# First attention of a two-block network: the probability pipeline made one step deeper

## The chip, the cores and the metric

The kernel runs on one core of one Trainium2 chip, in one launch. The metric is device time in microseconds (us), lower is better. The core has five engines that run their own instruction streams and meet only at semaphores: TensorE (PE: matrix products and transposes), VectorE (DVE), ScalarE (ACT), GpSimd (POOL) and SyncE (SP, which here only issues transfers).

## The reference

The network has two blocks on one sequence of 512 tokens and 1,024 features: a recurrent and convolutional mixer with a retrieval layer, and then two attention layers, each with a SwiGLU. The change concerns only the first attention, which has 16 heads of 64 features in 4 groups. Each head's output is a gated sum of three attentions (cut to what matters; all eight key blocks are selected, so "sel" is a full causal attention):

```python
p_cmp = softmax(q @ k_cmp + bias)      # 31 compressed keys
p_sel = softmax(q @ k_sel + bias)      # all keys up to the query
p_win = softmax(q @ k_win + bias)      # the last 256 keys
g = sigmoid(gl + b_gate)               # (tokens, heads, 3)
o = g[..., 0:1] * (p_cmp @ v_cmp) + g[..., 1:2] * (p_sel @ v_sel) + g[..., 2:3] * (p_win @ v_win)
```

## The kernel before

**Items and steps.** Heads are handled in pairs ("half" 0 and 1), eight pairs ("items") in all. Each pair takes four steps, one for each tile of 128 queries, `qt` = 0 to 3, so there are `STEPS` = 32 steps. A step's size follows `qt`: the sel scores are 128, 256, 384 and 512 wide, the win scores 128, 256, 384 and 384, and the cmp scores 31. Below, "step 3" is a step with `qt` = 3, and "iteration i" is the turn of an engine's loop whose `s` has `qt` = i.

**The work of a step s**, in the order in which data flows through it:
1. `scores(s)` on TensorE: six products (three branches for two heads) into PSUM banks 0 to 3. There is one set of these banks, so each product waits until DVE has read the last step's (`bank_read`).
2. `row_max(s)` on DVE: six reductions that add the bias, write to the probability buffer `pA[s % 3]` in SBUF and give the row maxima (L1611).
3. `exponentials(s)` on ACT: six Exp instructions in place, with row sums (L1664).
4. `inverse(s)` on DVE: the inverted sums times the gates, three small instructions (L1627, L1629, L1633), which raise `inv_ready`.
5. `scale(s)` on DVE: three multiplications for half 0 (L1640: sel, win, cmp) and one for half 1 (L1644: sel). At the same time GpSimd does half 1's win and cmp (L1696).
6. `turn(s)` on TensorE: the scaled probabilities are transposed block by block into PSUM banks 4, 5 and 7, in chunks of four blocks (L1556). Step 0 has 4 wide blocks, step 1 has 8, step 2 has 12 and step 3 has 14, and each has two narrow cmp blocks; that gives 2, 3, 4 and 4 chunks. A chunk may be written only when the chunk three before it in the running count has been copied out of the same bank.
7. The copies of the chunks to SBUF (`ptA`, two buffers): all but a step's last chunk by ACT (`copies`, L1589), the last chunk by DVE (`last_copy`, L1592, and for step 3 first L1589, since its last chunk has two wide blocks too).
8. `values(s)` on TensorE: products of values and turned probabilities (L1570). After an item's step 3 ACT drains the output (`drain`, L1678).

**The order is written by hand.** An engine runs its own list strictly in order:
- TensorE in iteration s: `scores(s+1)`, `values(s-2)`, `turn(s-1)`.
- DVE in iteration s: `row_max(s)`, `last_copy(s-2)`, `inverse(s-1)`, `scale(s-1)`.
- ACT in iteration s: `exponentials(s)`, `copies(s-1)`, `drain` if step s-2 ended an item.

Before the first of DVE's reductions stands one tiny copy (L381). When the attention ends, the output projection begins on TensorE (L563).

Of the kernel before, what the change touches and what calls it, by code (L numbers as in the profile page):

```python
# [21 lines left out]
P = 128  # L22
ALU = mybir.AluOpType
ACT = mybir.ActivationFunctionType
# [139 lines left out]
def program(nc, t):  # L164

    with ExitStack() as ctx:
# [123 lines left out]
        cin = wide.take(2, CMP_POS // 2, NKV * NCMP + 1)  # L290
        hid_bias = wide.take(2, 2, 1)
        a2 = Region(after)
        pA, ptA = a2.take(3, 2 * 928), a2.take(2, 16 * P)
        mxA, denA, invA = a2.take(3, 2, 3), a2.take(3, 2, 3), a2.take(3, 2, 3)
# [1202 lines left out]
        DVE_ORDER = (("sel", 0), ("win", 0), ("cmp", 0), ("sel", 1), ("win", 1), ("cmp", 1))  # L1497
        READS_BEFORE = (1, 4, 3, 6, 3, 6)
        SCORES_BEFORE = (1, 5, 5, 2, 6, 6)

# [33 lines left out]
        def nsa_pe(pe):  # L1534
# [6 lines left out]
                        pe.wait_ge(LA.bank_read, PER * (s - 1) + READS_BEFORE[x])  # L1541
                    pe.matmul(b.scores, b.q, b.keys, start=True, stop=True).then_inc(LA.scores_ready, 1)  # L1542

            def turn(s):
                for c, chunk in enumerate(turn_chunks(s)):
                    no = chunk_no(s) + c
                    turns = len(TURN_BANKS)
                    if no - turns in bank_of:
                        chunk_copied(pe, *bank_of[no - turns])
                    bank_of[no] = s, c  # L1550
                    other = max(half for half, _ in chunk)
                    pe.wait_ge(LA.scaled, 2 * s + 1 + other)
                    if other:
                        pe.wait_ge(LA.scaled_rest, s + 1)
                    for x, (_, (at, width, _)) in enumerate(chunk):
                        tr = pe.transpose(ps[0:width, turn_bank(no), P * x:P * x + P], pA[:, s % 3, at:at + width], ident)  # L1556
                    tr.then_inc(LA.turned, 1)

            def values(s):
# [24 lines left out]

# [9 lines left out]

        def nsa_dve(dve, step):

            def row_max(s):

                it, qt = divmod(s, TT)
                if qt == 0:  # L1600
                    dve.wait_ge(LA.tab_in[it % 2], 16 * 2 * (it // 2 + 1))
                if s >= 3:
                    dve.wait_ge(LA.turned, chunk_no(s - 2))
                    dve.wait_ge(LA.exp_done, s - 2)
                if s:
                    dve.wait_ge(LA.bank_read, PER * s)
                apart(dve)
                for x, (name, half) in enumerate(DVE_ORDER):
                    b = branches(s, half)[name]
                    dve.wait_ge(LA.scores_ready, PER * s + SCORES_BEFORE[x])  # L1610
                    dve.tensor_tensor_reduce(  # L1611
                        out=pA[:, s % 3, b.at:b.at + b.width], in0=b.scores, in1=b.tab, scale=1.0, scalar=-FLOOR,
                        op0=ALU.add, op1=ALU.min,
                        accum_out=mxA[:, s % 3, half, b.slot:b.slot + 1]).then_inc(LA.bank_read, 1)

            def last_copy(s):
                c = len(turn_chunks(s)) - 1
                dve.wait_ge(LA.turned, chunk_no(s + 1))
                if s >= 2:
                    dve.wait_ge(LA.pv_done, s - 1)  # L1620
                copy_chunk(dve.tensor_copy, s, c, LA.last_copied)

            def inverse(s):
                it, qt = divmod(s, TT)
                dve.wait_ge(LA.exp_done, s + 1)
                den, inv = denA[:, s % 3], invA[:, s % 3]
                step.do(dve.tensor_scalar(den, den, 1e-30, None, ALU.max))  # L1627
                step.settle()
                step.do(dve.reciprocal(inv, den))  # L1629
                step.settle()  # L1630
                h0 = heads(it)[0]
                gates = gateA[:, qt, :].rearrange("p (a b) -> p a b", b=3)[:, h0:h0 + GR + 1:GR, :]
                dve.tensor_tensor(inv, inv, gates, ALU.mult).then_inc(LA.inv_ready, 1)  # L1633

            def scale(s):
                sides = [branches(s, half) for half in range(2)]
                dve.wait_ge(LA.inv_ready, s + 1)
                for b in sides[0].values():
                    pr = pA[:, s % 3, b.at:b.at + b.width]
                    ins = dve.tensor_scalar(pr, pr, invA[:, s % 3, 0, b.slot:b.slot + 1], None, ALU.mult)  # L1640
                ins.then_inc(LA.scaled, 1)
                b = sides[1]["sel"]
                pr = pA[:, s % 3, b.at:b.at + b.width]
                dve.tensor_scalar(pr, pr, invA[:, s % 3, 1, 1:2], None, ALU.mult).then_inc(LA.scaled, 1)  # L1644

            for s in range(STEPS + 2):
                if s < STEPS:
                    row_max(s)
                if s >= 2:
                    last_copy(s - 2)  # L1650
                if 1 <= s <= STEPS:
                    inverse(s - 1)
                    scale(s - 1)

        def nsa_act(act):

            def exponentials(s):
                if s >= 3:
                    act.wait_ge(LA.inv_ready, s - 2)
                for half in range(2):  # L1660
                    act.wait_ge(LA.bank_read, PER * s + 3 * half + 3)
                    for b in branches(s, half).values():
                        pr = pA[:, s % 3, b.at:b.at + b.width]
                        ins = act.activation(pr, pr, ACT.Exp, bias=mxA[:, s % 3, half, b.slot:b.slot + 1], scale=-1.0,  # L1664
                                             accum_out=denA[:, s % 3, half, b.slot:b.slot + 1])
                ins.then_inc(LA.exp_done, 1)

            def copies(s):
# [9 lines left out]
                act.copy(attn[:, it, :].rearrange("p (a t) -> p a t", a=TT),  # L1678
                         bank(OUT_BANK).rearrange("p (a t) -> p a t", a=TT)[:, :, ::-1]).then_inc(LA.o_drained, 1)

            for s in range(STEPS + 2):
                if s < STEPS:
                    exponentials(s)
                if 1 <= s <= STEPS:
                    copies(s - 1)
                if s >= 2 and (s - 2) % TT == TT - 1:
                    drain((s - 2) // TT)

        def nsa_pool(pool):

            for s in range(STEPS):
                pool.wait_ge(LA.inv_ready, s + 1)
                side = branches(s, 1)
                for b in (side["win"], side["cmp"]):
                    pr = pA[:, s % 3, b.at:b.at + b.width]
# [1359 lines left out]
```

## Time and profile before

| | us |
|---|---|
| median of three runs | 2896.09 |
| lowest and highest | 2893.24, 2896.78 |
| span of the profiled execution | 2893.6 |
| first matmul of the first attention's scores, from the span's start | 1605.67 |
| first matmul after the first attention | 1761.23 |

The page of the profile gives the profiled execution by its span, 2893.6 us; no separate time for what lies around it is listed. "Busy" is the time in which an engine executes; a matmul's end is modelled, so a busy TensorE may still be waiting inside a group. A group's start is that of its first instruction; the distance from one group's start to the next one's start is what the first really took on its engine. In brackets behind a row stands the idle time ahead of it and what ended that.

### The profile page before, as it was taken

Reading aid. Unit: us, or ns where it says so; the run is one execution under the profiler, and the core shown is the slowest. Engines: PE = TensorE matmul, PEld = TensorE weight load, DVE = VectorE, ACT = ScalarE, POOL = GpSimd, SP = SyncE. Lnnn points to the kernel's source line nnn. Section 1 sums busy time; section 2 is a strip of 40 time slices with the busy share of each in tenths; the row PEclk is TensorE's granted clock in tenths of the full one; section 3 lists DMA queues with packets and bytes.
Section 4 is the critical chain, followed back from the end, with each engine's and each line's share of the span. In section 5 each row is a group of like instructions: output and inputs, shape, how many; then the busy total and the mean of one; then the engine's idle time right before and its main releaser. Section 6 shows DMA issues by size and latency. Waiting matters only on the chain.

```text
span 2893.6 us, 35834 instructions
## 1 busy us (share of the span) xinstructions
PE 2703.8 (93%) x12080; PEld 1725.0 (60%) x12080; DVE 1888.1 (65%) x4922; ACT 845.0 (29%) x1654; POOL 1183.9 (41%) x837
## 2 busy tenths in 40 slices
PE   8998999999877877799999999999999999999999
PEld 3374454444323322244447777888888877788887
DVE  8998788888888888778766896544223336554411
ACT  4732211111111111121123785222232127522222
POOL 5314444444444444344440233444434434444443
PEclk9999999999999999999999999999999999999999
DMA  4169999999999999999997221232323222222332
GB/s 131 61 236 370 420 412 421 420 420 420 422 421 410 415 421 412 421 419 420 420 420 239 60 69 54 97 97 94 107 87 100 92 68 66 66 95 95 102 101 79
DMA packets 130309, 700.39 MB, mean 242 GB/s; under 512 B 16694, under 2 KB 28886, under 8 KB 64343
## 3 DMA queue, kind: packets, MB, share of 16 engines
q0 software_dynamic: 74352, 543.04, 45.6%
q1 hardware_dynamic: 54760, 153.30, 16.0%
q10 hardware_dynamic: 1072, 2.41, 0.2%
q8 instruction: 75, 1.23, 0.2%
q14 instruction: 50, 0.41, 0.0%
HBM read 696.41 MB, written 2.28 MB: 241 GB/s over the span
## 4 chain that ended last, share of the span: by engine, by line
PE 49%; DMA 19%; issue 14%; DVE 9%; POOL 7%; ACT 1%; POOLq 0%; DVEq 0%; SPq 0%; ACTq 0%
DMA arena<-in_peer_uv,arena 18%; PE ps L543 16%; PE ps L883 14%; POOL w_lo L420 6%; PE ps L2363 3%; DVE arena L1216 2%; PE ps L911 2%; PE ps L795 1%; PE ps L1556 1%; PE ps L1570 1%; DVE arena L1227 1%; PE ps L852 1%; PE ps L1542 1%; PE ps L2023 1%; DMA ring<-in_a_in 1%
## 5 line engine op out<-in xcount | busy, mean ns | idle before, releaser
L883 PE MATMUL ps<-arena 128*128 128x512 f32 x2048 | 952.0, 609 | 145.6 <-DVE arena L1227 144.7
L1350 POOL DMA_INDIRECT arena<-in_peer_uv,arena x512 | 568.9, 1111 | 785.6 <-PE ps L883 723.8
L883 PEld LDWEIGHTS ps<-arena 128*128 128x128 f32 x2048 | 380.8, 192 | 653.2 <-issue 383.2
L1216 DVE CUSTOM_DVE_ANT_0 arena<-arena,sq 128x1024 f32<-128x1024 f32 x512 | 607.1, 1223 | 195.0 <-DMA arena<-in_peer_uv,arena 190.8
L420 POOL TENSOR_TENSOR w_lo<-ring,w_hi 128x1024 fp32r<-128x1024 f32 (+1 forms) x156 | 407.2, 2610 | 514.9 <-ACT w_hi L433 514.9
L543 PE MATMUL ps<-n_hi,w_hi 128*128 128x512 f32 x992 | 387.5, 391 | 0.5 <-issue 0.3
L543 PE MATMUL ps<-n_hi,w_lo 128*128 128x512 f32 x992 | 386.0, 389 | 0.0
L543 PE MATMUL ps<-n_lo,w_hi 128*128 128x512 f32 x992 | 381.9, 389 | 0.2 <-DVE n_lo L470 0.2
L1043 ACT ACTIVATE dots_gel<-dots_gel,tok_scale 128x2 f32<-128x2 f32 x256 | 75.6, 295 | 1006.7 <-DVE dots_gel L1216 1006.6
L433 ACT CAST w_hi<-ring 128x1024 fp32r<-128x1024 f32 (+1 forms) x156 | 174.6, 1119 | 644.3 <-PE ps L543 644.3
L543 PEld LDWEIGHTS ps<-n_hi,w_hi 128*128 128x128 f32 x992 | 186.2, 188 | 40.9 <-issue 2.4
L543 PEld LDWEIGHTS ps<-n_lo,w_hi 128*128 128x128 f32 x992 | 186.2, 188 | 40.1 <-DVE n_lo L470 0.8
L543 PEld LDWEIGHTS ps<-n_hi,w_lo 128*128 128x128 f32 x992 | 186.2, 188 | 38.5
L1227 DVE TENSOR_SCALAR arena<-consts,dots_gel,tcmp 128x128 f32<-128x128 f32 x512 | 160.4, 365 | 29.2 <-ACT dots_gel L1043 13.8
L599 DVE TENSOR_TENSOR h<-ps,h 128x512 f32<-128x512 f32 x32 | 22.1, 691 | 218.9 <-PE ps L543 218.9
L1425 DVE TENSOR_TENSOR arena<-ps,rstd 128x512 f32<-128x512 f32 x44 | 30.4, 692 | 200.4 <-PE ps L543 200.4
L543 PE MATMUL ps<-hid_hi,w_hi 128*128 128x512 f32 x352 | 137.1, 389 | 1.3 <-POOL w_lo L420 1.3
L543 PE MATMUL ps<-hid_lo,w_hi 128*128 128x512 f32 x352 | 137.0, 389 | 0.0
L543 PE MATMUL ps<-hid_hi,w_lo 128*128 128x512 f32 x352 | 136.9, 389 | 0.0
L2363 PE MATMUL ps<-n,ring 128*128 128x512 f32 x256 | 113.9, 602 | 8.2 <-DMA ring<-in_w_in 7.5
L1696 POOL TENSOR_SCALAR arena<-arena 128x384 f32<-128x384 f32 (+2 forms) x64 | 53.1, 839 | 163.2 <-DVE arena L1633 163.2
L911 PE MATMUL ps<-n,ring 128*128 128x384 f32 x320 | 111.9, 486 | 0.0
(366 smaller groups left out, 3619.2 us busy)
## 6 DMA issues: line engine op xcount, KB each, us to landing
ring<-in_a_up SPq DMA_DIRECT2D x44, 512.0 KB, 3.5
ring<-in_b_up SPq DMA_DIRECT2D x44, 512.0 KB, 3.5
ring<-in_a_in SPq DMA_DIRECT2D x40, 512.0 KB, 7.2
ring<-in_b_q SPq DMA_DIRECT2D x24, 512.0 KB, 3.4
ring<-in_a_down SPq DMA_DIRECT2D x16, 704.0 KB, 3.9
ring<-in_b_down SPq DMA_DIRECT2D x16, 704.0 KB, 4.0
ring<-in_w_in SPq DMA_DIRECT2D x16, 512.0 KB, 3.7
arena<-in_peer_uv,arena POOLq DMA_INDIRECT x512
```

The lines of the kernel that those rows point to most:

```text
L420: pool.tensor_tensor(w_lo[:, j % 2, 0:kt * P], ring[:, j, 0:kt * P], w_hi[:, j % 2, 0:kt * P], ALU.subtract).then_inc(split_lo, 1)
L433: act.copy(w_hi[:, j % 2, 0:kt * P], ring[:, j, 0:kt * P]).then_inc(split_hi, 1)
L543: mm = pe.matmul(bank(j // 2 if two else j), w[:, j % 2, cols], r[:, x, :], start=no == 0 and not (two and j % 2), stop=no == len(passes) ...
L883: mm = pe.matmul(bank(2 * (tt % 2) + q), diag[:, no % DIAGS, r, :], uvrow[p][r][:, D + 512 * q:D + 512 * q + 512], start=slot + r == 0, st ...
L911: mm = pe.matmul(ps[:, p % 2, 0:EARLY], ring[:, p % RING, k * P:(k + 1) * P], n[:, k, 0:EARLY], start=k == 0, stop=k == DK - 1)
L1043: act.activation(gel[:, p, :], dots[:, p, :], ACT.Gelu_apprx_tanh, scale=tok_scale[:, tt:tt + 1]).then_inc(gel_ready, 1)
L1216: ins = dve.tensor_tensor_reduce(out=u, in0=u, in1=ntok[:, tt, :], scale=1.0, scalar=0.0, op0=ALU.mult, op1=ALU.add, accum_out=dots[:, p, ...
L1227: ins = dve.tensor_scalar(diag[:, no % DIAGS, r, :], ident, gel[:, p, r:r + 1], gate_now[:, slot + r:slot + r + 1], ALU.mult, ALU.mult)
L1350: pool.indirect_dma_start(uvrow[p][r], None, t["peer_uv"], bass.IndirectOffsetOnAxis(ap=expert_id[:, tt, slot + r:slot + r + 1], axis=0)). ...
L1425: dve.tensor_tensor(gated[:, pr, :], bank(2 * pr + 1), rstd[:, :], ALU.mult).then_inc(tile_drained, 1)
L1696: ins = pool.tensor_scalar(pr, pr, invA[:, s % 3, 1, b.slot:b.slot + 1], None, ALU.mult)
L2363: mm = pe.matmul(bank(u % RING), ring[:, u % RING, k * P:(k + 1) * P], ns[k], start=k == 0, stop=k == DK - 1)
```

## The change

Four probability buffers instead of three; the transposes of a step run one iteration later than before, and are split in two parts around the values and the scores; GpSimd takes half 1's sel and win instead of its win and cmp; DVE takes both halves' cmp in one `tensor_tensor`; DVE's reductions of half 1 come behind the last chunk's copy. The new orders are:
- TensorE in iteration s: `turn(s-2, 0)` (the chunks with blocks of half 0 only), `values(s-3)`, `scores(s+1)`, `turn(s-2, 1)` (the others).
- DVE in iteration s: `row_max(s, 0)`, `last_copy(s-3)`, `row_max(s, 1)`, `inverse(s-1)`, `scale(s-1)`.
- ACT in iteration s: `exponentials(s)`, `drain` if step s-3 ended an item, `copies(s-2)`.

```diff
+        SLOTS_A = 4
-        pA, ptA = a2.take(3, 2 * 928), a2.take(2, 16 * P)
+        pA, ptA = a2.take(SLOTS_A, 2 * 928), a2.take(2, 16 * P)
...
-            def turn(s):
+            def turn(s, later):
                 for c, chunk in enumerate(turn_chunks(s)):
+                    other = max(half for half, _ in chunk)
+                    if other != later:
+                        continue
                     no = chunk_no(s) + c
                     turns = len(TURN_BANKS)
                     if no - turns in bank_of:
                         chunk_copied(pe, *bank_of[no - turns])
                     bank_of[no] = s, c
-                    other = max(half for half, _ in chunk)
-                    pe.wait_ge(LA.scaled, 2 * s + 1 + other)
+                    pe.wait_ge(LA.scaled, s + 1)
                     if other:
                         pe.wait_ge(LA.scaled_rest, s + 1)
...
             scores(0)
-            for s in range(STEPS + 2):
+            for s in range(STEPS + 3):
+                if 2 <= s <= STEPS + 1:
+                    turn(s - 2, 0)
+                if s >= 3:
+                    values(s - 3)
                 if s + 1 < STEPS:
                     scores(s + 1)
-                if s >= 2:
-                    values(s - 2)
-                if 1 <= s <= STEPS:
-                    turn(s - 1)
+                if 2 <= s <= STEPS + 1:
+                    turn(s - 2, 1)
...
             def scale(s):
-                sides = [branches(s, half) for half in range(2)]
+                side = branches(s, 0)
                 dve.wait_ge(LA.inv_ready, s + 1)
-                for b in sides[0].values():
-                    pr = pA[:, s % 3, b.at:b.at + b.width]
-                    ins = dve.tensor_scalar(pr, pr, invA[:, s % 3, 0, b.slot:b.slot + 1], None, ALU.mult)
-                ins.then_inc(LA.scaled, 1)
-                b = sides[1]["sel"]
-                pr = pA[:, s % 3, b.at:b.at + b.width]
-                dve.tensor_scalar(pr, pr, invA[:, s % 3, 1, 1:2], None, ALU.mult).then_inc(LA.scaled, 1)
-
-            for s in range(STEPS + 2):
+                for b in (side["sel"], side["win"]):
+                    pr = pA[:, s % SLOTS_A, b.at:b.at + b.width]
+                    dve.tensor_scalar(pr, pr, invA[:, s % SLOTS_A, 0, b.slot:b.slot + 1], None, ALU.mult)
+                pr = pA[:, s % SLOTS_A, :].rearrange("p (h c) -> p h c", h=2)[:, :, 896:896 + NCMP]
+                dve.tensor_tensor(pr, pr, invA[:, s % SLOTS_A, :, 0:1].broadcast_to([P, 2, NCMP]), ALU.mult).then_inc(LA.scaled, 1)
+
+            for s in range(STEPS + 3):
                 if s < STEPS:
-                    row_max(s)
-                if s >= 2:
-                    last_copy(s - 2)
+                    row_max(s, 0)
+                if s >= 3:
+                    last_copy(s - 3)
+                if s < STEPS:
+                    row_max(s, 1)
                 if 1 <= s <= STEPS:
                     inverse(s - 1)
                     scale(s - 1)
...
-            for s in range(STEPS + 2):
+            for s in range(STEPS + 3):
                 if s < STEPS:
                     exponentials(s)
-                if 1 <= s <= STEPS:
-                    copies(s - 1)
-                if s >= 2 and (s - 2) % TT == TT - 1:
-                    drain((s - 2) // TT)
+                if s >= 3 and (s - 3) % TT == TT - 1:
+                    drain((s - 3) // TT)
+                if 2 <= s <= STEPS + 1:
+                    copies(s - 2)
...
                 side = branches(s, 1)
-                for b in (side["win"], side["cmp"]):
-                    pr = pA[:, s % 3, b.at:b.at + b.width]
-                    ins = pool.tensor_scalar(pr, pr, invA[:, s % 3, 1, b.slot:b.slot + 1], None, ALU.mult)
+                for b in (side["sel"], side["win"]):
+                    pr = pA[:, s % SLOTS_A, b.at:b.at + b.width]
+                    ins = pool.tensor_scalar(pr, pr, invA[:, s % SLOTS_A, 1, b.slot:b.slot + 1], None, ALU.mult)
                 ins.then_inc(LA.scaled_rest, 1)
```

## Rows read from the trace of the kernel before

**Rows 1.** The page: the span.

```profile
span 2893.6 us, 35834 instructions
```

**Rows 2.** Windows: one item of four steps; busy us of each engine, granted clock, DMA.

```profile
1657.90:1676.50 18.60, 18.00 (x187) 13.90 (x187) 16.93 (x87) 15.98 (x59) 6.62 (x9) 1.00 0.16 54
```

**Rows 3.** Chain of waits: start us, us, what; first scores, and first turn of a step 2.

```profile
1605.67 0.86 PE ps L1542 x12
...
1620.66 1.77 PE ps L1556 x14
```

**Rows 4.** Timeline of TensorE, one item: start us, us, line, shape, [idle before].

```profile
1676.49 1.77 PE L1556 MATMUL ps<-consts,arena 128*128 128x128 f32 x14 [0.50 <-DVE arena L1640]
1678.19 1.27 PE L1542 MATMUL ps<-arena 64*128 64x256 f32 x12
1679.39 1.91 PE L1570 MATMUL ps<-arena 128*64 128x128 f32 x28
1681.23 2.05 PE L1556 MATMUL ps<-consts,arena 128*128 128x128 f32 x16
1683.20 1.70 PE L1542 MATMUL ps<-arena 64*128 64x384 f32 x12
1684.83 2.12 PE L1570 MATMUL ps<-arena 128*64 128x128 f32 x32
1686.89 0.88 PE L1556 MATMUL ps<-consts,arena 128*128 128x128 f32 x6
1687.69 1.91 PE L1542 MATMUL ps<-arena 64*128 64x512 f32 x12
1689.54 1.02 PE L1570 MATMUL ps<-arena 128*64 128x128 f32 x12
1690.49 1.31 PE L1556 MATMUL ps<-consts,arena 128*128 128x128 f32 x10
1691.73 1.46 PE L1542 MATMUL ps<-arena 64*128 64x128 f32 x12
1693.13 1.46 PE L1570 MATMUL ps<-arena 128*64 128x128 f32 x20
1695.10 1.07 PE L1556 MATMUL ps<-consts,arena 128*128 128x128 f32 x8 [0.51 <-DVE arena L1640]
```

**Rows 5.** Timeline of the last two steps and the stage's end.

```profile
1750.93 1.77 PE L1556 MATMUL ps<-consts,arena 128*128 128x128 f32 x14 [0.64 <-DVE arena L1640]
...
1755.47 2.02 PE L1556 MATMUL ps<-consts,arena 128*128 128x128 f32 x16
...
1757.53 0.42 DVE L1589 COPY arena<-ps 128x256 f32<-128x256 f32 x1 [1.94 <-PE ps L1556]
...
1758.42 2.12 PE L1570 MATMUL ps<-arena 128*64 128x128 f32 x32 [0.93 <-DVE arena L1592]
...
1761.23 4.13 PE L563 MATMUL ps<-sq,ring 128*128 128x512 f32 x9 [0.69 <-ACT sq L1678]
```

**Rows 6.** Timeline of ACT: a copy, the drain, a step 3's first Exp, the next copy.

```profile
1687.64 0.59 ACT L1589 COPY arena<-ps 128x512 f32<-128x512 f32 x1 [1.54 <-PE ps L1556]
1688.12 0.59 ACT L1678 COPY sq<-ps 128x512 f32<-128x512 f32 x1
...
1692.55 0.73 ACT L1664 ACTIVATE arena<-arena 128x512 f32<-128x512 f32 x1
...
1695.82 0.59 ACT L1589 COPY arena<-ps 128x512 f32<-128x512 f32 x1
```

**Rows 7.** Chain of waits near the stage's end: from ACT's copies to TensorE.

```profile
1751.66 1.57 ACT arena L1589 x3
1753.23 0.25 issue
```

**Rows 8.** Line L1644 on DVE: duration ns min/median/max, forms.

```profile
L1644 DVE TENSOR_SCALAR arena<-arena x32: 274/514/687, 1611.0 to 1754.9; 128x128 f32<-128x128 f32 x8, 128x256 f32<-128x256 f32 x8, 128x384 f32<-128x384 f32 x8, 128x512 f32<-128x512 f32 x8
```

**Rows 9.** One step's scaling: timelines of DVE and GpSimd, GpSimd's wide instruction by form.

```profile
1674.78 1.56 DVE L1640 TENSOR_SCALAR arena<-arena 128x384 f32<-128x384 f32 x3
...
1674.84 1.94 POOL L1696 TENSOR_SCALAR arena<-arena 128x384 f32<-128x384 f32 x2 [3.14 <-DVE arena L1633]
...
L1696 POOL TENSOR_SCALAR arena<-arena 128x384 f32<-128x384 f32 x1 | 1.5, 1470 | 3.1 <-DVE arena L1633 3.1
```

**Rows 10.** GpSimd by form, whole kernel: the same operation 512 wide, another line.

```profile
L1873 POOL TENSOR_SCALAR arena<-arena 128x512 f32<-128x512 f32 x8 | 14.9, 1856 | 6.4 <-DVE arena L1856 6.4
```

More of the change, by code:

```diff
@@ L292, in program @@
         a2 = Region(after)
-        pA, ptA = a2.take(3, 2 * 928), a2.take(2, 16 * P)
-        mxA, denA, invA = a2.take(3, 2, 3), a2.take(3, 2, 3), a2.take(3, 2, 3)
+        SLOTS_A = 4
+        pA, ptA = a2.take(SLOTS_A, 2 * 928), a2.take(2, 16 * P)
+        mxA, denA, invA = (a2.take(SLOTS_A, 2, 3) for _ in range(3))
         onehot, rowbuf = low[:, 3, :], skT.rearrange("p a b -> p (a b)")
@@ L1496, in program @@
         PE_ORDER = (("sel", 0), ("sel", 1), ("win", 0), ("win", 1), ("cmp", 0), ("cmp", 1))
-        DVE_ORDER = (("sel", 0), ("win", 0), ("cmp", 0), ("sel", 1), ("win", 1), ("cmp", 1))
         READS_BEFORE = (1, 4, 3, 6, 3, 6)
@@ L1555, in turn @@
                     for x, (_, (at, width, _)) in enumerate(chunk):
-                        tr = pe.transpose(ps[0:width, turn_bank(no), P * x:P * x + P], pA[:, s % 3, at:at + width], ident)
+                        tr = pe.transpose(ps[0:width, turn_bank(no), P * x:P * x + P], pA[:, s % SLOTS_A, at:at + width], ident)
                     tr.then_inc(LA.turned, 1)
@@ L1595, in nsa_dve, with row_max @@
         def nsa_dve(dve, step):
-            def row_max(s):
+            def row_max(s, half):
                 it, qt = divmod(s, TT)
[L1600 to L1608, printed above, removed]
+                if not half:
+                    if qt == 0:
+                        dve.wait_ge(LA.tab_in[it % 2], 16 * 2 * (it // 2 + 1))
+                    if s >= SLOTS_A:
+                        dve.wait_ge(LA.turned, chunk_no(s - SLOTS_A + 1))
+                        dve.wait_ge(LA.exp_done, s - SLOTS_A + 1)
+                    if s:
+                        dve.wait_ge(LA.bank_read, PER * s)
+                    apart(dve)
+                for x, name in enumerate(("sel", "win", "cmp")):
                     b = branches(s, half)[name]
-                    dve.wait_ge(LA.scores_ready, PER * s + SCORES_BEFORE[x])
+                    dve.wait_ge(LA.scores_ready, PER * s + SCORES_BEFORE[3 * half + x])
                     dve.tensor_tensor_reduce(
-                        out=pA[:, s % 3, b.at:b.at + b.width], in0=b.scores, in1=b.tab, scale=1.0, scalar=-FLOOR,
+                        out=pA[:, s % SLOTS_A, b.at:b.at + b.width], in0=b.scores, in1=b.tab, scale=1.0, scalar=-FLOOR,
                         op0=ALU.add, op1=ALU.min,
-                        accum_out=mxA[:, s % 3, half, b.slot:b.slot + 1]).then_inc(LA.bank_read, 1)
+                        accum_out=mxA[:, s % SLOTS_A, half, b.slot:b.slot + 1]).then_inc(LA.bank_read, 1)
             def last_copy(s):
@@ L1625, in inverse @@
                 dve.wait_ge(LA.exp_done, s + 1)
-                den, inv = denA[:, s % 3], invA[:, s % 3]
+                den, inv = denA[:, s % SLOTS_A], invA[:, s % SLOTS_A]
                 step.do(dve.tensor_scalar(den, den, 1e-30, None, ALU.max))
@@ L1657, in exponentials @@
             def exponentials(s):
-                if s >= 3:
-                    act.wait_ge(LA.inv_ready, s - 2)
+                if s >= SLOTS_A:
+                    act.wait_ge(LA.inv_ready, s - SLOTS_A + 1)
                 for half in range(2):
@@ L1662, in exponentials @@
                     for b in branches(s, half).values():
-                        pr = pA[:, s % 3, b.at:b.at + b.width]
-                        ins = act.activation(pr, pr, ACT.Exp, bias=mxA[:, s % 3, half, b.slot:b.slot + 1], scale=-1.0,
-                                             accum_out=denA[:, s % 3, half, b.slot:b.slot + 1])
+                        pr = pA[:, s % SLOTS_A, b.at:b.at + b.width]
+                        ins = act.activation(pr, pr, ACT.Exp, bias=mxA[:, s % SLOTS_A, half, b.slot:b.slot + 1], scale=-1.0,
+                                             accum_out=denA[:, s % SLOTS_A, half, b.slot:b.slot + 1])
                 ins.then_inc(LA.exp_done, 1)
```

2 lines of the change are left out of this document (1 added, 1 removed).

## The prediction

> **What bounds the kernel now.** I read the page's span first [rows 1]: 2893.6 us, 0.1% under the median of the runs (2896.09), so a difference worked out on the span can be added to the median as it stands. Then the chain of waits, for where the stage lies: from the first scores at 1605.67 [rows 3] to the next stage's first matmul at 1761.23 [rows 5] are 155.56 us. All the rest of the kernel is untouched, so the change can move 5% of the time at most.
>
> The stage is periodic. A step 2's turn starts at 1620.66 [rows 3], and the last item's at 1750.93 [rows 5]: seven periods of 18.61 us. The windows [rows 2] show that nobody is far from full in one: TensorE 18.00 busy of 18.60, DVE 16.93, ACT 15.98, GpSimd 6.62, and the clock at its upper level. But a busy TensorE hides waits inside its groups, so I take what each group costs from the distance between starts [rows 4]:
> - turns: 1.70 (step 2), 1.97 (step 3), 0.80 (step 0), 1.24 (step 1), together 5.71. A chunk of four wide blocks is 0.49 (1.97 / 4).
> - values: 1.84 (step 2), 2.06 (step 3), 0.95 (step 0), 1.46 (step 1), together 6.31.
> - scores: 1.20 (step 1, 1,086 columns), 1.63 (step 2, 1,598), 1.85 (step 3). Step 0's took 1.40 for only 574 columns; at 0.84 ns a column, the slope of the first two, it would take 0.77. The other 0.63 is waiting for DVE's reads of the banks. Unheld sum: 5.45.
>
> So TensorE has 17.47 us of work in a period. The other 1.14 us are that 0.63 and the 0.51 in which step 2's turn waits for DVE's scaling [rows 4]. That is all a deeper pipeline can win: 1.14 x 7 = 8.0 us, if it adds no wait of its own.
>
> **The change part by part.** A turn one iteration later no longer waits for scaling: minus 0.51. DVE reads half 1's scores while TensorE does values, so the next scores aren't held: minus 0.63. Now what the new order makes late.
>
> (a) *The last chunk's copy.* Before, scores (0.8 to 1.9 us) stood between the turn of a step's last chunk and its values, and hid the copy. Now the last chunk comes at the end of an iteration, and the next begins with `turn(s-2, 0)` and then these same values. Step 0 has no chunk of half 0 alone (its four wide blocks are two of each half), so in iteration 2 nothing stands between step 3's last chunk and step 3's values. The trace has this very sequence once, at the stage's end, where TensorE had nothing else to do: turn at 1755.47, two copies by DVE, values at 1758.42 after 0.93 us idle [rows 5]. Plus 0.93 per period. In the other iterations there is one copy less (some 0.3 less, so 0.6) against one chunk of 0.49 as cover: 0.1 to 0.15 each, where no longer wait swallows it.
>
> (b) *ACT's order.* ACT does the copies of step s-2 behind the Exps of step s, and the Exps of step s+1 behind those copies. Count from the end of step 3's last chunk, T = 0, with every duration from the rows. TensorE: wait 0.93, values(3) 2.06, scores(3) 1.85, first chunk of step 0 0.49: at 5.33. Only then can ACT copy this chunk, since it was turned in the late part. ACT: 0.10 to see it (the copy in rows 5 follows the end of its turn by less), 0.48 from copy to next instruction [rows 6], six Exps of step 3 in 3.27 (1692.55 to 1695.82) [rows 6], then step 1's first copy 0.59 and 0.25 until TensorE moves on an ACT copy (1753.23 to 1753.48) [rows 7]: 10.02. TensorE needs this copy, because step 2's first chunk goes to the bank of step 1's first chunk (three back). On its own path it would be there at 5.33 + 0.31 (rest of step 0's turn) + 0.49 + 0.15 + 0.95 + 0.77 + 0.75 = 8.75. Plus 1.27 per period, the largest term, and a new one: behind the waiting transpose stand values(1) and scores(1), and DVE and ACT live on those scores.
>
> (c) *The rest of the period.* Chunk 0.49, values(1) 1.46, scores(1) 1.20, rest of step 2's turn 1.21: 14.38. Step 3's first chunk needs the bank of step 2's second chunk, turned at 13.66 and copied at 13.66 + 0.10 + 0.59 + 0.25 = 14.60: plus 0.22, which covers (a) in this iteration. Then 0.49, values(2) 1.84, scores(2) 1.63, rest of step 3's turn 1.48: 20.04. Check: 17.47 + 0.93 + 0.15 + 1.27 + 0.22 = 20.04.
>
> (d) *DVE and GpSimd.* L1644 goes: 32 instructions with a median of 514 ns [rows 8], some 2 us a period. It lies beside TensorE's values and turns now, DVE has 1.7 us idle a period already [rows 2], and in the new chain (a to c) DVE appears only with its copies: priced at nothing. If DVE were the bound it would be worth up to 16 us. The joint cmp `tensor_tensor` has 62 columns for 31; the trace has no such form. From below, it costs what the narrow multiplication does now. From above: in the step shown DVE's three L1640 end at 1676.34 and GpSimd's first, 384 wide, at 1674.84 + 1.47 = 1676.31 [rows 9]; the narrow one, last of the three, is done only when GpSimd's is. GpSimd's first becomes step 3's sel, 512 wide, 1.86 for 1.47 [rows 9, 10]: up to 0.4 us more a period on DVE. I take this upper end, and it still costs nothing: about 2 us saved, 0.4 given back. GpSimd's own pair of step 3 takes 1.86 + 1.47 = 3.3 us and is needed a whole iteration later; at 0.39 for each 128 columns, the difference of the two, its four pairs make 9.8 us a period, of 18.6.
>
> The Trainium skill, "SBUF — State Buffer", section "Who interferes with whom", says that DVE and GpSimd share one port pair as an exclusive lock, and that a `tensor_tensor` with both inputs in SBUF contends with GpSimd's reads. By that the new instruction is held exactly as the old one; the ends 1676.34 and 1676.31 agree [rows 9]. By the rule the hold is the 0.4 of above, without it 0; the sum is the same either way, because DVE is off the chain.
>
> (e) *The ends.* The fourth buffer itself costs nothing. From the last item's first chunk of step 2 to the next stage's first matmul: before 10.30 [rows 5]; after 0.49 + 1.46 + 1.21 + 0.22 + 0.49 + 1.84 + 1.48 + 0.93 + 2.81 (values of step 3 to L563, 1758.42 to 1761.23) = 10.9. From the first scores to the first chunk of step 2: before 14.99; after it follows ACT's four first sets of Exps and one copy, by my estimate 14.5, give or take 1. The ends cancel to +0.1.
>
> Sum: 7 x (20.04 - 18.61) + 0.1 = +10.1 us, so 2906.2.
>
> **The rivals.**
> - *Only the copy is exposed* (a without b). If ACT's excursion were 1.3 us shorter than I add up, or DVE's relief let the Exps start early, the period would be 17.47 + 0.93 + 3 x 0.15 = 18.85, and the time +1.7, 2897.8: no change. For it: (b) is a sum of small latencies and I have each from one place. Against: the order on ACT is fixed, and step 3's Exps can't start before step 0's chunk is turned.
> - *It is what a deeper pipeline should be* (the other side). TensorE never waits: 17.47 a period, minus 8.0, plus 0.1: 2888.2. One mechanism decides: that the last chunk is copied within the time of what stands ahead of its values. It would have to take under 0.49 us, and nothing at all in iteration 2; the 0.93 in rows 5 speaks against it. Only if unheld matmuls run faster than the distances in rows 4 say could this come out.
> - *GpSimd's wider work holds DVE.* If the joint cmp waited for both of GpSimd's instructions (3.3 us instead of 1.9) in step 3, DVE would be 1.4 late for step 1's first reductions and step 2's last copy, where I count some 0.4 of slack: 1 us a period more, +17, 2913. For it: the lock-like ends in rows 9. Against: there the narrow one waited for the first only.
> - *It does nothing*: the waits removed and made cancel. That is the first rival's number.
>
> **How the numbers follow.** My forecast 0.62 (2903 to 2909.5: 0.1 to 0.2 us on each of the four latencies, seven times, and the ends' 1 us); exposed copy only 0.18; faster 0.08; held by GpSimd 0.07; the rest, 0.05, beyond either end. Predicted time 2906. The range 2897 to 2912 takes in the forecast and the first rival. A measurement can tell about 0.2% (5.8 us) from no change. Slower: 0.57 of the forecast's 0.62, the GpSimd case, and half of the rest: 0.67. Same: 0.18, 0.05 and 0.01: 0.24. Faster 0.09.
>
> **What the new profile would show.** The distance of the first chunks of step 2 from item to item: 20.0 (18.85 or 17.5 for the rivals). Idle of 0.9 ahead of step 3's values, released by DVE's copy; about 1.3 ahead of step 2's first chunk, released by ACT's copy (L1589's place); no wait for scaling, and scores of step 0 in about 0.8. On ACT a wait of over 1 us for step 0's chunk ahead of step 3's Exps. DVE busy down by some 1.5 a period with more idle, GpSimd busy up to about 10 a period. I am wrong if that wait on ACT is missing, or if TensorE's groups are shorter than their distances here.

## The result and the profile after

The changed kernel takes 2905.63 us (median of five runs, 2903.45 to 2908.45) against 2896.09 (with two more executions of the kernel before, five in all, the median is the same and the lowest is 2890.80). The ratio is 1.0038, 95% interval 1.0028 to 1.0049: slower by 8 to 14 us. The profiled execution spans 2901.3 us. That is only 7.7 over the one of before, because the untouched part ahead of the stage happened to be 4.3 us shorter (first scores at 1601.33 for 1605.67); over all profiled kernels here that start lies anywhere from 1601.3 to 1605.7. So I compare the stage itself, from the first scores to the next stage's first matmul: 1768.98 - 1601.33 = 167.65 us for 155.56, or +12.1.

Timeline of TensorE in the changed kernel, a little over one item (L1558 is the turn, L1572 values, L1542 scores; it answers to [rows 4]):

```profile
1687.07 2.12 PE L1572 MATMUL ps<-arena 128*64 128x128 f32 x32 [0.93 <-DVE arena L1596]
1689.12 1.91 PE L1542 MATMUL ps<-arena 64*128 64x512 f32 x12
1690.97 1.31 PE L1558 MATMUL ps<-consts,arena 128*128 128x128 f32 x10
1692.39 1.03 PE L1572 MATMUL ps<-arena 128*64 128x128 f32 x12
1693.35 0.86 PE L1542 MATMUL ps<-arena 64*128 64x128 f32 x12
1694.14 0.88 PE L1558 MATMUL ps<-consts,arena 128*128 128x128 f32 x6
1696.05 0.66 PE L1558 MATMUL ps<-consts,arena 128*128 128x128 f32 x4 [1.03 <-ACT arena L1593]
1696.64 1.47 PE L1572 MATMUL ps<-arena 128*64 128x128 f32 x20
1698.03 1.27 PE L1542 MATMUL ps<-arena 64*128 64x256 f32 x12
1699.24 1.99 PE L1558 MATMUL ps<-consts,arena 128*128 128x128 f32 x14
1701.26 1.91 PE L1572 MATMUL ps<-arena 128*64 128x128 f32 x28
...
1707.19 2.13 PE L1572 MATMUL ps<-arena 128*64 128x128 f32 x32 [0.93 <-DVE arena L1596]
```

The period is 1707.19 - 1687.07 = 20.12 us, for 18.61. The two waits in brackets are the two that the prediction named. The first, ahead of step 3's values, ends with DVE's copy of the last chunk. The second, ahead of step 2's first chunk, ends with ACT's copy of step 1's. Scores of step 0 now take 0.79 (1693.35 to 1694.14), for 1.40 before, and no wait of TensorE's ends with scaling.

Timeline of ACT in the changed kernel (L1669 Exps, L1593 copies, L1683 drain; it answers to [rows 6]):

```profile
1689.53 0.56 ACT L1683 COPY sq<-ps 128x512 f32<-128x512 f32 x1
1691.72 0.59 ACT L1593 COPY arena<-ps 128x512 f32<-128x512 f32 x1 [1.62 <-PE ps L1558]
1692.20 0.73 ACT L1669 ACTIVATE arena<-arena 128x512 f32<-128x512 f32 x1
...
1695.42 1.05 ACT L1593 COPY arena<-ps 128x512 f32<-128x512 f32 x2
```

ACT stands idle for 1.62 us until step 0's chunk is turned, and only then starts step 3's Exps; step 1's copies, for which TensorE waits, follow 3.22 us later.

Windows of one item in the changed kernel (the columns of [rows 2]):

```profile
1669.01:1689.12 20.11, 17.98 (x188) 13.76 (x186) 15.94 (x82) 16.15 (x59) 9.03 (x9) 1.00 0.17 48
```

DVE is busy for 1.0 us less and idle for 4.2; GpSimd is busy for 2.4 more. TensorE and ACT work as much as before and wait more.

The end, from the last item's first chunk of step 2 to the next stage, took 12.58 us (1756.40 to 1768.98), for 10.30 before. Timeline and windows (the third number from the end is TensorE's granted clock as a share of 2.4 GHz) of the changed kernel there:

```profile
1756.40 1.12 PE L1558 MATMUL ps<-consts,arena 128*128 128x128 f32 x4 [1.82 <-ACT arena L1593]
1757.45 2.48 PE L1572 MATMUL ps<-arena 128*64 128x128 f32 x20
...
1756.00:1757.40 1.40, 1.00 (x4) 0.72 (x4) 1.30 (x5) 0.83 (x2) 1.40 (x2) 0.60 0.00 0
1757.40:1759.80 2.40, 2.40 (x21) 1.87 (x20) 0.34 (x2) 0.59 (x1) 2.40 (x2) 0.52 0.02 7
```

With no more scores to do, TensorE idled for 1.82 us, and behind that its clock was granted at half, 1.2 GHz, until 1759.7: values(1) took 2.41 us instead of 1.40. The idle alone doesn't decide it: in e5_narrow the same group stood behind the same 1.82 us of idle, and the clock stayed at 1.00.

### The profile page after: what moved, and what is told of

The parts are those of the page before. It is cut to its first block, busy times and chain, and to the rows that moved or that the text cites. A ratio compares the mean times of both kernels' runs of the same rounds, so it can differ in the third digit from the quotient of the medians.

```text
span 2901.3 us, 35800 instructions
## 1 busy us (share of the span) xinstructions
PE 2707.6 (93%) x12080; PEld 1726.6 (60%) x12080; DVE 1879.3 (65%) x4890; ACT 846.3 (29%) x1654; POOL 1204.7 (42%) x837
## 3 DMA queue, kind: packets, MB, share of 16 engines
q10 hardware_dynamic: 1072, 2.41, 0.3%
## 4 chain that ended last, share of the span: by engine, by line
PE 49%; DMA 19%; issue 14%; DVE 8%; POOL 7%; ACT 2%; POOLq 0%; DVEq 0%; ACTq 0%; SPq 0%
DMA arena<-in_peer_uv,arena 18%; PE ps L544 16%; PE ps L884 14%; POOL w_lo L421 6%; PE ps L2368 3%; DVE arena L1217 3%; PE ps L912 2%; PE ps L1572 2%; PE ps L1558 1%; PE ps L1542 1%; DVE arena L1228 1%; PE ps L796 1%; ACT arena L1669 1%; PE ps L2028 1%; PE ps L774 1%
## 5 line engine op out<-in xcount | busy, mean ns | idle before, releaser
L1701 POOL TENSOR_SCALAR arena<-arena 128x128 f32<-128x128 f32 (+3 forms) x64 | 72.3, 1140 | 150.6 <-DVE arena L1638 150.6
```

Source lines behind the costliest of these rows:

```text
L1701: ins = pool.tensor_scalar(pr, pr, invA[:, s % SLOTS_A, 1, b.slot:b.slot + 1], None, ALU.mult)
```

## The experiments

Every ratio is against the kernel before in runs on the same chip. "Period" is the distance between the scores of step 3 in two items, "stage" is as above. The kernel before had medians of 2892.7 to 2893.4 us beside the experiments, so rows are compared by their ratios, not by their times. Period and stage are of one profiled execution each. Six of these had some microseconds at half clock in the stage: the changed kernel, e4_early0 and e6_oldscale near its end, e7_mid, e8_deep_oldscale and e9_tail in the first item. So a difference of up to 3 us between two stages can be the clock's; the periods, taken from later items, are free of it.

| kernel | us | ratio (95%) | period | stage |
|---|---|---|---|---|
| before | | | 18.61 | 155.6 |
| changed | 2905.63 | 1.0038 (1.0028 to 1.0049) | 20.12 | 167.7 |
| e1_deeper | 2891.29 | 1.0000 (0.9991 to 1.0009) | 18.07 | 153.9 |
| e2_split | 2901.81 | 1.0027 (1.0015 to 1.0038) | 19.73 | 164.6 |
| e3_between | 2904.69 | 1.0039 (1.0025 to 1.0052) | 20.12 | 166.1 |
| e4_early0 | 2902.91 | 1.0029 (1.0019 to 1.0040) | 19.76 | 165.2 |
| e5_narrow | 2904.47 | 1.0041 (1.0025 to 1.0056) | 20.12 | 166.5 |
| e6_oldscale | 2908.02 | 1.0053 (1.0040 to 1.0067) | 20.35 | 170.0 |
| e7_mid | 2895.20 | 1.0005 (0.9996 to 1.0014) | 18.62 | 158.3 |
| e8_deep_oldscale | 2897.40 | 1.0017 (1.0007 to 1.0026) | 18.40 | 159.1 |
| e9_tail | 2889.98 | 0.9991 (0.9982 to 1.0000) | 18.08 | 152.0 |
| e10_early | 2891.84 | 0.9997 (0.9988 to 1.0006) | 18.56 | 154.7 |

**e1_deeper: the depth with the old orders.**

```diff
-                if 2 <= s <= STEPS + 1:
-                    turn(s - 2, 0)
-                if s >= 3:
-                    values(s - 3)
                 if s + 1 < STEPS:
                     scores(s + 1)
+                if s >= 3:
+                    values(s - 3)
                 if 2 <= s <= STEPS + 1:
-                    turn(s - 2, 1)
+                    turn(s - 2)
```

and on DVE `row_max(s, 0)`, `row_max(s, 1)`, `last_copy(s - 3)`.

> The changed kernel with the old orders one step deeper: TensorE in iteration s does scores(s+1), values(s-3), turn(s-2) whole; DVE does both halves of row_max(s), then last_copy(s-3). Four buffers and the new scaling stay. My theory (the cost is the place of the last chunk's copy and of ACT's Exps behind step 0's copy): scores stand between a last chunk and its values again, so the 0.93 us idle ahead of step 3's values goes; ACT still waits for step 0's chunk ahead of step 3's Exps, and TensorE then waits some 0.7 us for step 1's copies ahead of values(1). Period 17.5 + 0.7 = 18.2 us, stage some 3 us shorter than in the kernel before, time about 2893. Rival (depth itself or the new scaling is what costs): period stays near 20, time about 2905.

Measured: period 18.07, 2 us under that of the changed kernel. The depth isn't what costs, the order is. (The edit takes back two orders at once, TensorE's and DVE's split reductions; they weren't separated.) The 0.93 us are gone inside a period. The time falls back to that of the kernel before, not 3 us under it: of the 3.8 us that seven shorter periods give, the end takes 3.5 back (1755.29 - 1734.11 = 21.18 us from the last scores of step 3 to the next stage, for 1761.23 - 1743.53 = 17.70 before). The stage of the profile is 1.7 us shorter; I had 3. Timeline of TensorE, e1_deeper, a period and the last items:

```profile
1689.39 1.47 PE L1570 MATMUL ps<-arena 128*64 128x128 f32 x20 [0.41 <-ACT arena L1589]
...
1743.61 1.47 PE L1570 MATMUL ps<-arena 128*64 128x128 f32 x20 [1.91 <-ACT arena L1589]
1745.01 1.80 PE L1556 MATMUL ps<-consts,arena 128*128 128x128 f32 x14
1747.67 1.91 PE L1570 MATMUL ps<-arena 128*64 128x128 f32 x28 [0.87 <-ACT arena L1589]
1749.51 2.05 PE L1556 MATMUL ps<-consts,arena 128*128 128x128 f32 x16
1752.48 2.12 PE L1570 MATMUL ps<-arena 128*64 128x128 f32 x32 [0.93 <-DVE arena L1592]
```

Ahead of values(1) TensorE waits 0.41 (I had 0.7), and at the end, without scores between, every values pays for its copies.

**e2_split: the new scaling alone, in the kernel before** (the diff of `scale` and `nsa_pool`, with `s % 3`, and of `turn`'s wait for the scaling).

> The kernel before with the new division of the scaling alone (GpSimd sel and win of half 1, one tensor_tensor for both cmp), no depth. My theory: DVE gains about 0.35 us in each scaling and reaches step 2's scaling earlier, but the turn right behind it must now wait for GpSimd's two wide instructions (2.7 us for step 2, 3.1 for step 3): about 0.7 and 0.6 us of wait a period against 0.51 before, and 0.35 less of waiting in scores. Period 18.9 to 19.0 us, time 2898 to 2900. Rival (DVE is the bound, so its relief is a gain): period 18.0 or less, time under 2892. Rival (the scaling is the whole loss of the change): period 20, time 2905.

Measured: period 19.73, 0.7 over my forecast's upper end. TensorE waited for GpSimd 0.91 us at the second chunk of step 2 and 0.64 at that of step 3, as bracketed by the timeline of e2_split:

```profile
1698.59 1.28 PE L1556 MATMUL ps<-consts,arena 128*128 128x128 f32 x10 [0.91 <-POOL arena L1694]
...
1704.15 1.50 PE L1556 MATMUL ps<-consts,arena 128*128 128x128 f32 x12 [0.64 <-POOL arena L1694]
```

The place was right, the sizes too small: by the distances of starts the two turns took 1.05 and 0.76 us more than their work, where I had 0.7 and 0.6. Another 0.15 stood ahead of that turn of step 2, for DVE, and 0.27 in the scores of step 0. By itself the new scaling costs three quarters of what the whole change does (9.0 us of stage for 12.1), but in the changed kernel no wait ends with it; the losses don't add.

**e3_between: the early chunk's copy between the halves' Exps.**

```diff
                 for half in range(2):
...
+                    if not half and s >= 2 and (s - 2) % TT:
+                        copies(s - 2, [0])
...
```

(`copies` now takes the chunks to be copied, and its usual call leaves the early one out.)

> The changed kernel, but ACT copies the early chunk (the first one of steps 1 to 3) between the Exps of the two halves instead of behind both. Theory 'bank': TensorE's wait of 1.1 us ahead of step 2's first chunk is for that bank alone, so it goes: period 19.0 us, time about 2898. Theory 'ACT is late' (mine): the wait is gone from there, but values(1) right behind it need step 1's second copy, which ACT does behind all Exps of step 3; it only moves by 0.5 us of copy. The wait reappears ahead of values(1), 1.2 us long; period 20.0 to 20.2, time 2904 to 2906.

Measured: same time and period as the changed kernel. The bank came free, but the wait didn't move whole to values(1), as I had it: it split in two. Timelines of TensorE and of DVE's last scaling of step 2, e3_between:

```profile
1698.97 0.63 PE L1558 MATMUL ps<-consts,arena 128*128 128x128 f32 x4 [0.38 <-DVE arena L1647]
1700.16 1.47 PE L1572 MATMUL ps<-arena 128*64 128x128 f32 x20 [0.56 <-ACT arena L1593]
...
1698.61 0.21 DVE L1647 TENSOR_TENSOR arena<-arena 128x62 f32<-128x62 f32 x1
```

Step 2's first chunk still waits 0.38 us, now for DVE's scaling of step 2, and values(1) wait 0.56 for ACT, where I had 1.2. In the changed kernel this scaling ends at 1695.03 + 0.21 = 1695.24. By the 0.15 us from its end to the chunk here, it alone would have held the chunk until 1695.39, so 0.45 of the 1.11 us hide a second wait behind the one for ACT. But values(1) start at almost the same place either way (7.45 us behind the scores of step 3 here, 7.52 in the changed kernel), and the period is the same: what sets it is ACT's lateness with step 3's Exps and with both copies behind them, not one bank.

**e4_early0: step 0's wide chunk in the early part.**

```diff
-                    if other != later:
+                    if (other if s % TT or c else 0) != later:
```

> The changed kernel, but step 0's wide chunk is turned in the early part of its iteration (ahead of step 3's values) instead of the late one. My theory: it covers 0.49 of the 0.93 us that the last copy exposes, and ACT has it copied before it needs to start step 3's Exps, which then wait for DVE's reductions only and start 0.5 us earlier. TensorE's idle ahead of values(3) falls to about 0.44, ACT's wait of 1.6 us for step 0's chunk goes. One loss of 0.5 a period goes with both, since they lie in one chain: period 19.6, time about 2902. Rival (the two terms are independent and both fall): period 19.1, time 2898.5. Rival (neither lies on the chain): 20.1, 2905.

Measured: period 19.76, 0.36 less, idle ahead of values(3) 0.47 for 0.93, and step 3's Exps wait for DVE's reductions (1.26 us) and not for the chunk: most of the 1.62 us that ACT waited in the changed kernel it would have waited anyway. Less than one loss went, not two (the wait ahead of step 2's first chunk is still 0.90): they are links of one chain. I had 0.5.

**e5_narrow: two narrow `tensor_scalar` for the joint `tensor_tensor`.**

```diff
-                pr = pA[:, s % SLOTS_A, :].rearrange("p (h c) -> p h c", h=2)[:, :, 896:896 + NCMP]
-                dve.tensor_tensor(pr, pr, invA[:, s % SLOTS_A, :, 0:1].broadcast_to([P, 2, NCMP]), ALU.mult).then_inc(LA.scaled, 1)
+                for half in range(2):
+                    b = branches(s, half)["cmp"]
+                    pr = pA[:, s % SLOTS_A, b.at:b.at + b.width]
+                    ins = dve.tensor_scalar(pr, pr, invA[:, s % SLOTS_A, half, 0:1], None, ALU.mult)
+                ins.then_inc(LA.scaled, 1)
```

> The changed kernel with two narrow multiplications by a scalar operand (tensor_scalar, 31 columns) for both cmp parts in place of the joint tensor_tensor of 62 columns, which took 0.21 us in the changed kernel while GpSimd was working. Theory 'form': a tensor_scalar between SBUF and SBUF is held while GpSimd's first instruction runs, a tensor_tensor isn't; the first narrow one of step 3 ends with GpSimd's 512 wide one, 1.8 to 1.9 us behind the start of the scaling. Rival 'order': the hold in the kernel before came from something else (its place as third, or the instruction behind it), and the narrow ones take about 0.2 us. Either way DVE is off the chain: period 20.1 us, time 2904 to 2908. If DVE were on it, plus 0.4 to 0.8 us a period, 3 to 6 us more.

Measured: same period and time. Timelines of DVE and GpSimd in step 3's scaling, first in the changed kernel (L1647 is the `tensor_tensor`):

```profile
1697.27 1.25 DVE L1645 TENSOR_SCALAR arena<-arena 128x512 f32<-128x512 f32 x2
1698.44 0.21 DVE L1647 TENSOR_TENSOR arena<-arena 128x62 f32<-128x62 f32 x1
...
1697.33 3.08 POOL L1701 TENSOR_SCALAR arena<-arena 128x512 f32<-128x512 f32 x2 [0.55 <-DVE arena L1638]
```

and in e5_narrow, with the first of the two narrow ones by itself, DVE's next reduction, and GpSimd by form:

```profile
1699.48 1.25 DVE L1645 TENSOR_SCALAR arena<-arena 128x512 f32<-128x512 f32 x2
1700.65 0.78 DVE L1649 TENSOR_SCALAR arena<-arena 128x31 f32<-128x31 f32 x2
...
1700.65 0.23 DVE L1649 TENSOR_SCALAR arena<-arena 128x31 f32<-128x31 f32 x1
...
1701.00 0.43 DVE L1616 CUSTOM_DVE_ANT_0 arena<-ps,arena 128x256 f32<-128x256 f32 x1
...
1699.54 3.08 POOL L1704 TENSOR_SCALAR arena<-arena 128x512 f32<-128x512 f32 x2 [0.66 <-DVE arena L1638]
...
L1704 POOL TENSOR_SCALAR arena<-arena 128x512 f32<-128x512 f32 x1 | 1.9, 1858 | 0.7 <-DVE arena L1638 0.7
```

The pair of narrow ones ends at 1701.43, GpSimd's 512 wide one at 1699.54 + 1.86 = 1701.40. But it is the second narrow one that ends there; the first took 0.23 us, and I had the first. In steps 0 to 2 the first is held as I expected: in step 2 it took 0.57 us and ended with GpSimd's 384 wide one, where the `tensor_tensor` in the same place took 0.21. So "form" holds there, and in step 3 only for the second. And "held" is the wrong picture of DVE: its next reduction started at 1701.00, 0.4 us before the narrow one's end, and 1.52 us behind the start of the scaling (1.50 in the changed kernel, 1697.27 to 1698.77). What comes late is the narrow instruction's end, and with it its signal (the turn in [rows 4] starts at 1676.49, 0.15 us behind such an end); the engine goes on. So e5_narrow hardly delays DVE, and the equal period doesn't show by itself that DVE is off the chain.

**e6_oldscale: the changed kernel with the old scaling.**

> The changed kernel with the scaling divided as before (DVE half 0 and half 1's sel, GpSimd half 1's win and cmp); orders and four buffers as changed. My theory: TensorE waits for ACT and for the last copy, not for scaling, in this order; DVE has over 4 us idle a period and takes 1 to 1.3 us of it: period 20.1 us, time 2904 to 2908. Rival (the wider work on GpSimd is what makes the changed kernel slow): period falls to 19.0 or less, time under 2898.

Measured: period 20.35, 0.23 more. DVE's scaling of step 2 ends later, so step 1's last copy does, and values(1) start 0.22 later behind the first chunk (1699.36 - 1698.55 = 0.81 for 0.59). The interval of the ratio touches that of the changed kernel; the periods of the two profiles are clear. So the new scaling isn't what makes the change slow, it helps it a little in this order.

**e7_mid: step 1's copies between the halves of step 3's Exps, on e1_deeper.**

```diff
+                    if not half and s % TT == TT - 1:
+                        copies(s - 2)
...
-                if 2 <= s <= STEPS + 1:
+                if 2 <= s <= STEPS + 1 and s % TT != TT - 1:
                     copies(s - 2)
```

> e1_deeper with one edit on ACT: step 1's two copies stand between the two halves of step 3's Exps instead of behind them. In e1_deeper TensorE waited 0.41 us for them ahead of values(1) in each period and 1.91 us in the last item. My theory: both go; the copies are done about 0.5 us ahead of need, and step 3's Exps end 1 us later than before, which nothing waits for while a step lies between. Period 17.6 to 17.7 us for 18.07, the end 1.5 us shorter: some 4 to 5 us less than e1_deeper, 0.2% under the kernel before. Rival (the late Exps of step 3 delay its inverse and scaling on DVE, which delays the next reductions and scores): the wait moves to scores, period 18.0 or more, same time as e1_deeper.

Measured: my theory fell; period 18.62. The wait ahead of values(1) went, but step 3's Exps end later, and DVE and TensorE both meet that. Timelines of DVE and TensorE, e7_mid:

```profile
1694.00 0.17 DVE L1628 TENSOR_SCALAR arena<-arena 128x6 f32<-128x6 f32 x1 [1.48 <-ACT arena L1664]
...
1696.64 0.40 PE L1556 MATMUL ps<-consts,arena 128*31 128x128 f32 x2 [0.59 <-ACT arena L1589]
```

DVE's inverse of step 3 waits 1.48 us, and step 2's last chunk waits 0.59 for its bank, since the copy of step 2's first chunk stands behind the late Exps. The scores of step 2 took 1.93 us for 1.63 besides, so the rival saw part of it; the end was 1.3 us shorter than in e1_deeper, near my 1.5. I had followed the copies that I moved, not those queued behind.

**e8_deep_oldscale: e1_deeper with the old scaling.**

> e1_deeper with the scaling divided as before. Here DVE matters: it had 17.2 us of work a period in the kernel before, and the period of e1_deeper is 18.07. My theory: DVE fits barely, the reductions of the next scores come later and TensorE's scores wait for them, 0.1 to 0.5 us a period: period 18.2 to 18.5, time 1 to 3 us over e1_deeper, so even with or just over the kernel before. Rival (DVE's relief is worth nothing at this depth): same as e1_deeper. Rival (GpSimd's wide work costs there too): faster than e1_deeper.

Measured: period 18.40, in the range, and 0.33 more than e1_deeper: the scores of step 1 took 1.73 us from start to start for 1.40, those of step 0 1.06 for 0.79. At this depth DVE's relief counts. The time is not in the range: by the ratios it is some 5 us over e1_deeper, where I had 1 to 3. Seven periods give 2.3; in the profile about 3 more lie in the first item, where TensorE had 6.8 us at half clock. Whether the other executions had that too isn't on record.

**e9_tail: another order in the last iterations, on e1_deeper.**

```diff
+                if STEPS <= s <= STEPS + 1:
+                    turn(s - 2)
                 if s >= 3:
                     values(s - 3)
-                if 2 <= s <= STEPS + 1:
+                if 2 <= s < STEPS:
                     turn(s - 2)
```

> e1_deeper with another order on TensorE in the last iterations only: turn(30) ahead of values(29), turn(31) ahead of values(30), so that no values stand directly behind the turn whose copies they need. In e1_deeper the last item paid 1.91, 0.87 and 0.93 us of idle ahead of its last three values. My theory: the period stays 18.07 and the end, from the last item's step 3 scores to the next stage, falls from 21.2 to 18.6 us: 2 to 3 us less than e1_deeper, 0.1% under the kernel before. Rival (the end is set by ACT's Exps and GpSimd's scaling of the last step): under 1 us less.

Measured: the end takes 1754.85 - 1736.12 = 18.73 us, for 21.18 in e1_deeper; period 18.08. Its ratio is the lowest of all, 0.1% under the kernel before and at the edge of what the runs can tell (0.9982 to 1.0000); it overlaps with those of e1_deeper and e10_early.

**e10_early: the kernel before, with an earlier signal.**

```diff
-                for b in sides[0].values():
+                for b in (sides[0]["sel"], sides[0]["win"]):
...
                 ins.then_inc(LA.scaled, 1)
+                pr = pA[:, s % 3, :].rearrange("p (h c) -> p h c", h=2)[:, :, 896:896 + NCMP]
+                dve.tensor_tensor(pr, pr, invA[:, s % 3, :, 0:1].broadcast_to([P, 2, NCMP]), ALU.mult)
```

and GpSimd does half 1's win alone.

> The kernel before, at its own depth and orders, with DVE raising the scaling's semaphore behind half 0's two wide parts (all that a step's first chunk reads), both narrow cmp parts in one tensor_tensor behind it, half 1's sel last; GpSimd does half 1's win alone. Theory: in the kernel before TensorE waited 0.51 us a period ahead of step 2's turn for the narrow part, which stood behind GpSimd's instruction for 0.57 us; now it doesn't wait, and DVE has no more work. Period 18.1 us, time 3 to 4 us under the kernel before. Rival (the second chunk is then held by half 1's sel, which ends no earlier): the wait moves to the second chunk; period 18.4 to 18.6, within 2 us of the kernel before.

Measured: the rival's number, by another wait. Period 18.56; step 2's turn starts without a wait, but from its start to the next group's are 2.17 us for 1.70. Only about 0.1 us of that stands at the second chunk. The rest stands ahead of the fourth, the narrow one. Timeline of TensorE's weight loads and of ACT, e10_early:

```profile
1692.82 0.14 PEld L1556 LDWEIGHTS ps<-consts,arena 128*31 128x31 f32 x2 [0.38 <-ACT arena L1589]
...
1692.19 1.54 ACT L1589 COPY arena<-ps 128x512 f32<-128x512 f32 x3
```

The fourth chunk goes to the first one's bank, and ACT copies the first only at 1692.19, behind its Exps. Free TensorE of DVE's scaling, and ACT's order is the next limit, in the kernel before too.

## Why the prediction was right

The time was forecast as 2906.2 and came as 2905.63, and the mechanism by its own steps:

- **TensorE's work, 17.47.** It held: from start to start, values and scores of a period took 11.72 us in the changed kernel, for 11.76 in my sum, and the waits counted below and 17.47 make the period.
- **(a) The last chunk's copy, 0.93.** Measured 0.93, from the same DVE line. e4_early0 halves it by putting one chunk ahead, e1_deeper takes it out.
- **(b) ACT's order, 1.27.** Measured 1.11 (1694.14 + 0.80 for the turn of step 1 makes 1694.94; the next chunk starts at 1696.05). e3_between shows that it is ACT's lateness and not the bank. What I left out: behind this wait 0.45 us for DVE's scaling of step 2 lie hidden, though I had said that a turn one iteration later no longer waits for scaling. It doesn't only because ACT comes later still.
- **(c) The rest, 0.22 and 0.15.** Measured, as distances of starts less the work of the blocks, 0.32 in the turn ahead of values(2), 0.18 in that ahead of values(0), and 0.10 in the chunk ahead of values(1). All waits: 2.64, and 17.47 + 2.64 = 20.11. Forecast 20.04, measured 20.12.
- **(d) DVE and GpSimd.** Off the chain in the changed kernel, as said: no wait of TensorE's there ends with scaling. But the `tensor_tensor` isn't held by GpSimd; the 0.4 us a period that I let it cost are 0. DVE's busy time still fell by 1.0 only, where I had 1.5, and GpSimd's rose to 9.03 and not to nearly 10, since its pair of step 3 took 3.08 us for my 3.3. And "DVE is off the chain" is not general: with the old scaling the same order is 0.23 a period slower (e6_oldscale), so I should have counted DVE's slack ahead of each last copy, which is a few tenths, and not only its 1.7 us idle a period.
- **(e) The ends, +0.1.** This was mis-sized: the head measured 14.23 (forecast 14.5, before 14.99), the end 12.58 (forecast 10.9, before 10.30). Together +1.5. The missing 1.7 at the end are mostly the half clock of this one profile: e5_narrow, the same order with the full clock there, has from the last scores of step 3 to the next stage 1769.59 - 1751.55 = 18.04, the changed kernel 1768.98 - 1749.48 = 19.50.

So the stage gained 7 x 1.51 + 1.5 = 12.1 us where I had 10.1, and without the half clock it would be some 10.6; the median moved by 9.5, and the ratio's interval, 8 to 14 us, holds them all. The period came within 0.08 us by the mechanism. That the total came within 1 us is luck on top of it: the interval is wider than that.

Of the rivals, the exposed copy alone (18.85) is excluded by the 1.03 us behind ACT. "GpSimd holds DVE" is excluded by the changed kernel's own trace: the `tensor_tensor` is done at 1698.65, 0.5 us before GpSimd's first instruction, and the next reductions start at 1698.77, while GpSimd works until 1700.41. "What a deeper pipeline should be" was a question of order: e1_deeper has the same depth and a period of 18.07. There remain its 0.41 for ACT and some 0.2 in scores; whether an order without them exists stays open, e7_mid wasn't it. No run takes ACT's late Exps away in the changed order, so the 1.11 us are assigned by the trace and by e3_between and e4_early0, not by a run without them.

## What to carry to other kernels

A deeper pipeline takes a wait away where a result is used, but in hand-written engine orders each consumer must also be kept away from the last thing that its input needs: write down, for each buffer and bank, what stands between the producer's last instruction and the first use, and look for the step where nothing does. An engine that does two kinds of work in order (Exps and copies here) passes the lateness of one on to the other; moving one instruction moves the wait, so follow the whole queue behind it before believing in a gain. And look at the last iterations by themselves: without new work between them they pay every latency that the steady state hides.

## What the runs showed of the hardware

- A narrow DVE `tensor_scalar` (31 columns) from SBUF to SBUF, third in the scaling, ended 0.04 us behind GpSimd's running instruction in all 32 places of the kernel before ([rows 9] has one). In e5_narrow it did so in steps 0 to 2, but in step 3, beside a 512 wide one of GpSimd's, it took 0.23 us and only the next narrow one ended with GpSimd's. DVE's reduction of PSUM started before that end (1701.00 for 1701.43).
- A DVE `tensor_tensor` of 62 columns, both inputs in SBUF, took 0.205 to 0.215 us in all 32 places of the changed kernel, also in the middle of GpSimd's 1.86 us. The Trainium skill, "SBUF — State Buffer", section "Who interferes with whom", says that a DVE instruction with two SBUF inputs contends with a GpSimd instruction that reads SBUF, and that a `tensor_scalar` can contend. Here the `tensor_scalar` does and the `tensor_tensor` doesn't. Its second input is a broadcast of one column, and whether that matters wasn't tried.
- GpSimd's pair of step 3 (sel 512 and win 384 wide) took 3.08 us; TensorE waited for it as soon as it stood right behind it (e2_split).
- An idle of 1.82 us on TensorE near the stage's end was followed by 3.4 us at half clock in the changed kernel's profile. In e5_narrow, with the same order and the same idle, the clock stayed at 1.00 and the end was 1.46 us shorter. Idle of about 1 us in each period left the clock at 1.00 in both. What made the difference stays open.
